# Layer 1 of a two-layer transformer: fifteen gate units computed as seven half-size products with their sums on VectorE, and 32 modulation tiles moved into the projections of layer 2

## The reference

```
m_lat = silu(c) @ w_mod + b_mod            # 6 x 1024 values a layer: shifts, scales, gates
m_ctx = silu(c_ctx) @ w_mod + b_mod
u_lat = h_lat * (1.0 + sc1) + sh1          # and u_ctx alike from m_ctx
pl, pc = u_lat @ w_in, u_ctx @ w_in        # queries, keys, values; pl[10], pc[10] are gate logits
# branches a, b, c, d: attention, Fourier mix, window attention, neighbourhood attention
gates = sigmoid(gate_logits)               # 4 branches x 1024 features
merged = sum over i of gates[i] * (branches[i] @ w_branch[i])
y = merged @ w_out
```

## Time and profile before

| | us |
|---|---|
| median of three executions | 2863.95 (2862.65 to 2864.39) |
| the profiled execution | 2864.46 |
| its span | 2862.6 |
| TensorE busy in the span | 2722.6 (95%) |
| VectorE busy | 1350.7 (47%) |
| ScalarE busy | 436.0 (15%) |

### The profile page before, as it was taken

The page is one execution under the profiler, slowest core; times in us unless marked ns, Lnnn a source line. Parts: engine busy times, 40 slices in busy tenths (PEclk is TensorE's granted clock), DMA queues, the critical chain, the costliest instruction groups (busy, mean ns, idle before and its releaser), DMA issues.

```text
span 2862.6 us, 42389 instructions
## 1 busy us (share of the span) xinstructions
PE 2722.6 (95%) x17586; PEld 1977.2 (69%) x17586; DVE 1350.7 (47%) x2753; ACT 436.0 (15%) x873; POOL 75.4 (3%) x137
## 2 busy tenths in 40 slices
PE   7999999998899899999988998899999999999998
PEld 3544444576666567788644444488788998988997
DVE  3856656442222233785411111179734764843763
ACT  0222220210000012231100000011422211122110
POOL 0100002000000000000100000000000000000000
PEclk9999999999999999999999999999999999999999
DMA  9623339379999985233899999954232444333441
GB/s 377 202 103 122 122 128 356 121 317 421 420 407 421 421 348 165 100 115 148 331 421 421 420 384 421 421 203 160 100 134 104 175 163 147 135 140 116 162 162 45
DMA packets 114765, 685.48 MB, mean 239 GB/s; under 512 B 20752, under 2 KB 22032, under 8 KB 39712
## 3 DMA queue, kind: packets, MB, share of 16 engines
q1 hardware_dynamic: 84144, 600.79, 53.1%
q0 software_dynamic: 16992, 69.54, 6.7%
q10 hardware_dynamic: 13456, 12.59, 1.7%
HBM read 679.46 MB, written 3.41 MB: 239 GB/s over the span
## 4 chain that ended last, share of the span: by engine, by line
PE 37%; DMA 14%; DVE 1%; issue 0%; ACT 0%; SPq 0%; DVEq 0%; ACTq 0%
PE ps L780 14%; DMA ring<-units 14%; PE ps L752 11%; PE ps L1527 2%; PE ps L1346 2%; PE ps L1222 2%; PE ps L1488 1%; DMA early_values<-arena 1%; PE ps L1358 0%; PE ps L1378 0%; PE ps L1088 0%; PE ps L815 0%; PE ps L789 0%; PE ps L798 0%; PE ps L1276 0%
## 5 line engine op out<-in xcount | busy, mean ns | idle before, releaser
L1222 PE MATMUL ps<-ring,arena 128*32 128x256 f32 x2928 | 359.8, 382 | 45.9 <-DMA ring<-units 44.4
L1207 PE MATMUL ps<-ring,arena 128*64 128x256 f32 x2960 | 339.3, 381 | 45.3 <-DMA ring<-units 45.1
L1207 PEld LDWEIGHTS ps<-ring,arena 128*64 128x64 f32 x2960 | 227.0, 137 | 148.7 <-issue 65.5
L1222 PEld LDWEIGHTS ps<-ring,arena 128*32 128x32 f32 x2928 | 175.2, 109 | 222.5 <-DMA ring<-units 90.9
L752 PE MATMUL ps<-h,ring 128*128 128x256 f32 (+1 forms) x992 | 246.0, 408 | 3.2 <-ACT h L1706 2.1
L1047 PE MATMUL ps<-u,ring 128*128 128x512 f32 (+1 forms) x544 | 235.1, 586 | 0.5 <-DVE arena L2345 0.5
L752 PEld LDWEIGHTS ps<-h,ring 128*128 128x128 f32 x992 | 186.7, 190 | 61.3 <-issue 34.7
L1047 PEld LDWEIGHTS ps<-u,ring 128*128 128x128 f32 x544 | 102.6, 191 | 126.7 <-issue 125.1
L2681 DVE COPY u<-ps 32x512 f32<-32x512 f32 (+1 forms) x128 | 70.9, 554 | 209.9 <-PE ps L1222 116.9
L752 PE MATMUL ps<-arena,ring 128*128 128x256 f32 x640 | 139.5, 379 | 1.3 <-DVE arena L3115 1.3
L752 PEld LDWEIGHTS ps<-arena,ring 128*128 128x128 f32 x640 | 121.4, 190 | 18.1 <-DVE arena L3008 1.7
(11 more groups left out here) (501 smaller groups left out, 3958.3 us busy)
## 6 DMA issues: line engine op xcount, KB each, us to landing
ring<-units SPq DMA_DIRECT2D x568, 1024.0 KB, 13.4
slots<-turned_mod POOLq DMA_DIRECT2D x62, 512.0 KB, 5.2
arena<-turned_mod POOLq DMA_DIRECT2D x18, 512.0 KB, 11.2
arena<-quarters ACTq DMA_DIRECT2D x32, 256.0 KB, 2.9
arena<-units POOLq DMA_DIRECT2D x7, 1024.0 KB, 7.2
h<-tokens SPq DMA_DIRECT2D x4, 512.0 KB, 12.2
arena<-neighbours ACTq DMA_DIRECT2D x32, 64.0 KB, 8.8
arena<-tokens ACTq DMA_DIRECT2D x1, 2048.0 KB, 14.2
```

What stands on the lines that cost most here:

```text
L1207: last = nc.tensor.matmul(ps[j * slots:(j + 1) * slots, bank, lo:lo + UC], lhsT[:, kt, 0:slots], row_of(w[j], kt), start=(kt == 0), stop=( ...
L1222: last = nc.tensor.matmul(ps[j % 4 * slots:(j % 4 + 1) * slots, banks[j // 4], 0:UC], lhsT[:, kt, 0:slots], row_of(w[j], kt), start=(kt == ...
```

## The change

Gate units 1 to 15 of layer 1 (512 tokens) are made by `gate_products`: the unit's eight row tiles are split in two halves, its 256 columns in two, and the 512 tokens in latent and context. Seven products of 4 matmuls with 256 columns each take the place of 16 matmuls with 512 columns. They use four banks, two of which (`wb`) also take the quarter's product, so that one waits for `gates_added`. VectorE sums each unit's weights one chunk ahead (`first_wide_sums`, `last_wide_sums`), the tokens once, and adds the results into `gate` in three steps (`early_blocks`, `add_fifth`, `late_blocks`). The sums lie in slots 4 to 7 of the ring, so units 16 to 34 go through slots 0 to 3 alone, and units 36 to 39 are loaded after the last merge.

The 32 tiles for the latent condition alone leave the chunks of layer 1. They are made at the nine places of layer 2's `prepare` (`MOD_AGAIN`), from a copy of the condition that is written to memory at the start and loaded back behind the parked unit 15; their loads stand at the end of GpSimd's program for layer 1, and only the three places of `slots` are left. Of the 48 other tiles, seven are made after `merge(15)`, ahead of the `w_out` residuals; `MOD_MIX` has one tile in each of chunks 0 to 11 and three in each of 12 to 15. The diff (declarations, the removed table `tile_places` and the matching removed lines are left out):

```diff
-MOD_MIX = (1,) + 10 * (3,) + (3, 10, 10, 9, 0)
+MOD_MIX = 12 * (1,) + 4 * (3,)
+MOD_AGAIN = (3, 4, 4, 4, 4, 4, 4, 4, 1)
+GATES, NARROW = 15, 35
+def slot_of(n):
+    return n % (RING // 2) if GATES < n < NARROW else n % RING
...
+        late_conditions = part(13824, 1, D)
...
+        wide_token_sums = [part(1024 * (i % 2), 4, S, of=ring[:, 4 + i // 2, :]) for i in range(4)]
+        wide_weight_sums = [[part(4 * P * i, 4, P, of=ring[:, 7 - q, :]) for i in range(4)] for q in range(2)]
+        gate_blocks = gate.rearrange("p j n -> p (j n)")
+        first_product_kept = small[:, 512:512 + S]
...
+            for n in range(2 * RING, NARROW + 5):
+                if n < 2 * RING + RING // 2:
+                    sp.wait_ge(units_used, n - RING + 1)
+                elif n <= NARROW:
+                    sp.wait_ge(units_used, n - RING // 2 + 1)
+                else:
+                    sp.wait_ge(merged_step, 16)
+                sp.dma_start(ring[:, slot_of(n), :], units[n]).then_inc(loaded[n % RING], 16)
+            gaps = [NARROW + 5] + [n + RING for n in units_to_parks()] + [n_units]
...
-            modulation_tiles(0, MOD_LATE + MOD_SLOTS)
-            pool.wait_ge(mixed, 24)
-            modulation_tiles(MOD_LATE + MOD_SLOTS, MOD_TILES)
+            pool.dma_start(ap["late_conditions"], conditions[0][0:1, 0, :]).then_inc(conditions_stored, 16)
+            modulation_tiles(0, MOD_BOTH)
+            pool.wait_ge(conditions_stored, 16)
             for l in range(DEPTH):
                 if l == 0:
-                    pool.wait_ge(mod_taken, MOD_TILES)
+                    pool.wait_ge(mod_taken, MOD_BOTH)
...
+                    pool.dma_start(late_conditions[:, 0, :], bass.AP(ap["late_conditions"].tensor, 0, [[0, P], [1, D]]))\
+                        .then_inc(conditions_loaded, 16)
...
+                if l == 0:
+                    modulation_tiles(MOD_BOTH, MOD_TILES)
...
+                def gate_products(c):
+                    w = unit()
+                    s, t = wide_weight_sums[c % 2], wide_token_sums
+                    def product(bank, half, lhsT, rhs):
+                        for k in range(4):
+                            last = nc.tensor.matmul(ps[:, bank, half * S:(half + 1) * S], lhsT[:, k, :], rhs[:, k, :],
+                                                    start=(k == 0), stop=(k == 3))
+                        return last
+                    pe.wait_ge(gate_kept, 2 * c)
+                    product(gb + 1, 0, w[:, 0:4, 0:P], u[:, 0:4, 0:S]).then_inc(wide_first_ready, 1)
+                    product(gb, 0, w[:, 4:8, 0:P], u[:, 4:8, 0:S])
+                    pe.wait_ge(wide_tokens_summed, 1)
+                    pe.wait_ge(wide_weights_summed, c)
+                    product(gb, 1, s[1], t[1]).then_inc(wide_early_ready, 1)
+                    attend(2 * c)
+                    pe.wait_ge(merged_step, c)
+                    product(wb + 1, 1, s[0], t[0]).then_inc(wide_fifth_ready, 1)
+                    product(wb, 1, s[2], t[2])
+                    product(wb, 0, s[3], u[:, 4:8, S:]).then_inc(wide_late_ready, 1)
+                    pe.wait_ge(wide_fifth_added, c)
+                    product(wb + 1, 0, w[:, 4:8, P:UC], t[3]).then_inc(units_used, 1)
...
+                    elif chunk:
+                        gate_products(chunk)
...
+                    elif l == 0:
+                        pe.wait_ge(gates_added, chunk)
...
+                    if l == 0 and chunk:
+                        exps(2 * chunk)
+                        act.wait_ge(wide_first_ready, chunk)
+                        A(first_product_kept, ps[:, gb + 1, 0:S], ACT.Copy).then_inc(wide_first_kept, 1)
+                        next_quarter(chunk)
+                        copies(2 * chunk)
+                        exps(2 * chunk + 1)
+                        copies(2 * chunk + 1)
+                        count.skip(units_used, 1)
+                        act.wait_ge(gates_added, chunk)
+                        A(gate[:, :, 0:T], gate[:, :, 0:T], ACT.Tanh, scale=0.5).then_inc(gate_kept, 2)
...
+                if l:
+                    dve.wait_ge(conditions_loaded, 32)
+                    modulated_tiles["from"] = late_conditions
 
                 def beside(place):
-                    if l == 0:
-                        modulation_tiles(MOD_PREPARE[place])
+                    modulation_tiles((MOD_AGAIN if l else MOD_PREPARE)[place])
...
+                first, second, third, fourth = [gate_blocks[:, n * S:(n + 1) * S] for n in range(4)]
+                def first_wide_sums(c):
+                    n, to = GATES + c, wide_weight_sums[c % 2]
+                    w = ring[:, slot_of(n), :].rearrange("p (k c) -> p k c", c=UC)
+                    dve.wait_ge(loaded[n % RING], 16 * (n // RING + 1))
+                    dve.wait_ge(units_used, max(n - 1, GATES))
+                    v.tensor_tensor(to[0], w[:, 0:4, P:UC], w[:, 4:8, P:UC], ALU.add).then_inc(dve_step, 1)
+                    v.tensor_tensor(to[2], w[:, 0:4, 0:P], w[:, 0:4, P:UC], ALU.subtract)
+                    dve.wait_ge(dve_step, at(dve_step))
+                def last_wide_sums(c):
+                    n, to = GATES + c, wide_weight_sums[c % 2]
+                    w = ring[:, slot_of(n), :].rearrange("p (k c) -> p k c", c=UC)
+                    link(v.tensor_tensor(to[1], to[0], w[:, 0:4, 0:P], ALU.subtract))
+                    v.tensor_tensor(to[3], w[:, 4:8, 0:P], to[1], ALU.subtract).then_inc(wide_weights_summed, 1)
+                def early_blocks(chunk):
+                    dve.wait_ge(merged_step, chunk)
+                    dve.wait_ge(wide_first_kept, at(wide_first_kept))
+                    dve.wait_ge(wide_early_ready, at(wide_early_ready))
+                    link(v.tensor_tensor(gate[:, :, 0:S], ps[:, gb, :].rearrange("p (a n) -> p a n", n=S),
+                                         wide(first_product_kept, [P, 2, S]), ALU.add))
+                def add_fifth():
+                    dve.wait_ge(wide_fifth_ready, at(wide_fifth_ready))
+                    v.tensor_tensor(second, third, ps[:, wb + 1, S:], ALU.add).then_inc(wide_fifth_added, 1)
+                def late_blocks():
+                    dve.wait_ge(wide_fifth_added, at(wide_fifth_added))
+                    dve.wait_ge(wide_late_ready, at(wide_late_ready))
+                    link(v.tensor_tensor(gate_blocks[:, S:3 * S], gate_blocks[:, S:3 * S], ps[:, wb, :], ALU.add))
+                    dve.wait_ge(units_used, at(units_used))
+                    count.skip(units_used, -1)
+                    link(v.tensor_tensor(fourth, third, ps[:, wb + 1, S:], ALU.add))
+                    v.tensor_tensor(third, third, ps[:, wb + 1, 0:S], ALU.add).then_inc(gates_added, 1)
...
-                        softmax(2 * chunk)
+                        softmax(2 * chunk, (lambda: first_wide_sums(chunk + 1)) if chunk < 15 else None)
+                        if chunk == 0:
+                            x, s = u, wide_token_sums
+                            link(v.tensor_tensor(s[0], x[:, 0:4, S:], x[:, 0:4, 0:S], ALU.subtract))
+                            link(v.tensor_tensor(s[1], x[:, 4:8, S:], s[0], ALU.subtract))
+                            v.tensor_tensor(s[2], x[:, 4:8, S:], x[:, 0:4, S:], ALU.subtract)
+                            v.tensor_tensor(s[3], x[:, 4:8, 0:S], s[1], ALU.subtract).then_inc(wide_tokens_summed, 1)
...
                         modulation_tiles(MOD_MIX[chunk] // 2, chunk)
                         if 2 * chunk < len(pairs):
                             keep(2 * chunk - 1)
-                        softmax(2 * chunk + 1)
+                        if chunk < 15:
+                            last_wide_sums(chunk + 1)
+                        if chunk:
+                            early_blocks(chunk)
+                            softmax(2 * chunk + 1, add_fifth)
+                            late_blocks()
+                        else:
+                            softmax(2 * chunk + 1)
                         modulation_tiles(MOD_MIX[chunk] - MOD_MIX[chunk] // 2, chunk)
...
                 merge(15)
+                if l == 0:
+                    modulation_tiles(MOD_BOTH - sum(MOD_PREPARE) - sum(MOD_MIX), 16)
```

More of the change, by code:

```diff
@@ L77 @@
 MOD_TILES = 80
-MOD_LATE = 51
-def tile_places(early, late):
-    used, last, places = {}, {}, []
-    for j in range(MOD_TILES):
-        s = j % early if j < MOD_LATE else (j - MOD_LATE) % (early + late)
-        used[s] = used.get(s, 0) + 1
-        places.append((s, used[s], last.get(s, -1)))
-        last[s] = j
-    return places
-TILE_PLACES = tile_places(MOD_SLOTS, 6)
-MOD_PREPARE = (2, 3, 4, 2, 2, 2, 2, 0, 0)
-MOD_MIX = (1,) + 10 * (3,) + (3, 10, 10, 9, 0)
+MOD_PREPARE = (2, 3, 4, 2, 2, 2, 2, 0, 0)
+MOD_MIX = 12 * (1,) + 4 * (3,)
[3 more added lines that the diff above has]
+    return n % (RING // 2) if GATES < n < NARROW else n % RING
 def constants():
@@ L346, in build @@
```

(30 more changed lines are left out.)

25 lines of the change are left out of this document (16 added, 9 removed).

## The result

The changed kernel took 2873.56 us (median of 6 runs, 2869.21 to 2876.56) beside 2863.97 us for the kernel before (6 runs, 2862.65 to 2866.3): a ratio of 1.0032, 95% interval 1.0021 to 1.0043. It is 9.6 us slower, 0.3%. Five more runs of it, taken beside the last version of experiment 7, had a median of 2874.07 us, 1.0041 [1.0028, 1.0055] of before. The first profiled execution (2869.21 us) was the fastest of the six, so I read a second one too (2873.09 us).

What follows compares the result with a forecast made beforehand. TensorE was taken to bound layer 1's chunks, with VectorE's work hidden in layer 2's prepare until it misses a date. 2864.46 - 21.4 + 0.5 + 22.0 + 1.8 = 2867.4, about 2867 us, range 2854 to 2880.

Steps and rivals of the forecast that it cites:

- likeliest case: Whole kernel: stall of 16 to 25 us and saving of 19 to 23 cancel, 2861 to 2872 us; chance 0.50.
- slower by loads: Layer 2's prepare: reloads of 5.5 us make the stall 30 us, time 2875; chance 0.15 beyond the forecast's own edge.
- Its own sign of being wrong: Profile after: a stall under 14 or over 30 us, or TensorE waiting for VectorE inside layer 1's chunks.
- Layer 1, -21.4: Layer 1's mixing: seven shorter products per gate unit, with changed waits, save 21.4 us in all.
- The two guesses in the sum: Layer 1: 2.0 us given back from waits for ScalarE's copies, 0.5 us allowed as loss in chunks 4 and 5.
- slower by VectorE in layer 1: Layer 1's chunks: VectorE's late dates lose 1 us in each of 11, saving 10, time 2878; chance 0.15.
- +0.5 for the extra issue: Start of layer 1: GpSimd's store of the condition ahead of the first tile counts in full, +0.5 us.
- The tiles behind `merge(15)`: End of layer 1's mixing: seven tiles take 17 us of VectorE, hidden behind `w_out`.
- The stall, 22.0: Layer 2's prepare: VectorE's chain of tiles and reloads ends at 1185.6 against 1163.55, so mixing starts 22 us late.
- Two bounds beside the sum: Layer 2's stall: 13 us with all reloads at 3.5 us and no crowding, 8 with none waiting.
- faster: Whole kernel: tiles land in 3.5 us, stall 13, saving 24, time 2856; decides under a 13.6 us stall; chance 0.15.
- The half clock, 1.8: Layer 2's first gate unit: after the stall TensorE's rows run at half clock, +1.8 us.

Runs made afterwards that it cites:

- experiment 7: Changed kernel's gate units, 22 tiles left in layer 2's gaps, five places; last version moves some tiles and reorders reloads against `planned`: 2844.96 us, 0.9939 of before.
- gates_only: Changed kernel without the 32 late tiles of layer 2 and their loads, output not the reference's: 2841.14 us, 0.9926 of the kernel before.
- planned: Changed kernel's gate units, but 58 tiles made in layer 1 and 22 in layer 2's gaps, with five places: 2851.54 us, 0.9963 of the kernel before.
- tiles_only: Kernel before with only the tiles moved as in the change, its gate units as before: 2900.52 us, 1.0131 of the kernel before.
- no_reloads: Changed kernel loading only the first three of the 32 late tiles, all computed, output not the reference's: 2849.93 us, 0.9957 of the kernel before.
- fill_half: Changed kernel with filling products on TensorE ahead of layer 2's first gate unit raised from 3 to 58: 2872.79 us, ratio 1.0032.
- fill_stall: Changed kernel with filling products on TensorE ahead of layer 2's first gate unit raised from 3 to 108: 2889.77 us, one run.

## Why the prediction was right or wrong

**The forecast as a whole.** 2867 against 2873.56: on the slower side of its likeliest case, inside the range, and slower by more than 0.2%, where I gave 0.38. Its own case ended at 2872 and a stall of 25; what happened is the rival "slower by loads", stall 30 and 2875, to which I gave 0.15. Its own sign of being wrong, a stall over 30, came in the second trace (31.0) and was just missed in the first (29.3). That the median stayed this near is in part luck: beside the 1.7 us of full clock in layer 1, both traces have 1.1 to 1.5 us less between `w_out` and the start of layer 2 (594.9 and 595.3 us against 596.4), as TensorE's waits for the ring there fell from 45.1 to 43.7 and 43.1 us. With the same layer 1 `gates_only` took 596.2 us and waited 45.3, so this moves between executions.

**Layer 1, -21.4: right.** The saving of the change itself in the trace is 22.8. The units took 12.25 us where the earlier trace rows gave 12.09, the bare wait 1.13 instead of 1.2. The two guesses in the sum were 1.4 short together: ScalarE's waits gave back 4.3 - 1.4 = 2.9 where I had 2.0, and the 0.5 us allowed for chunks 4 and 5 wasn't needed. The `gates_only` run, whose VectorE has fewer tiles in layer 1 as in the change, measures the whole of it, with the extra issue, as -21.5 against -20.9. The rival "slower by VectorE in layer 1" fell; VectorE even had room for a tile more in chunks 1 to 3 and 8 to 11 (`planned`).

**+0.5 for the extra issue: too small to see.** The start of mixing moved between 140.2 and 143.0 us from trace to trace. I put that down to when single tiles landed; no run shows it.

**The tiles behind `merge(15)`: hidden, as worked out.** VectorE waited once, and its fold was done 2.9 us ahead of TensorE, as before (522.29 - 519.39).

**The stall, 22.0: the term that was mis-sized.** It is 2.94 + 26.84 - 0.51 = 29.3 us in one trace and 2.68 + 28.83 - 0.51 = 31.0 in the other. The chain was the right one, and most of its links held. Of the 7.3 us that the first trace has more, 1.1 are the first keys and values, copied by 1085.49, which is 1112.3 before the shift of layer 2 by 26.8 us, where I had 1111.2; 1.0 lies in VectorE's other work; and 5.2 are waits for reloads, 22.9 instead of 7 x 2.33 + 1.4 = 17.7. Of these 5.2 the first group alone has 4.4: it waited 8.1 us (8.0 in the other trace) instead of 3.7. The other six waited 14.8 us together, and 14.0 was due. So the wrong step is "1.4 more for the first of them, whose reloads meet the crowded queues", put on top of "lands 4.4 us later, the median from 100 to 160 us". The reloads that the first group waited for were used 8.8 to 10.4 us after their issue (issued at 1080.18, 1082.37 and 1087.05, used at 1089.00, 1091.55 and 1097.48), the last one of the seven groups 3.6 us after it (1157.95 to 1161.58).

I took the price of a load from a stretch with a DMA share of 0.36 (100 to 160 us) and carried it, with 1.4 us for all crowding, to one in which ring, parked unit, constants, bias rows and condition come in at once. The earlier trace rows showed 0.49 as a mean over 79 us. The windows of the kernel before, in three pieces, would have shown me that its first 18 us are full (the first two pieces; the DMA share stands ahead of the last number):

```profile
1084.00:1102.00 18.00, 17.89 (x72) 10.99 (x70) 6.66 (x17) 0.60 (x1) 4.87 (x8) 1.00 0.98 308
1102.00:1127.00 25.00, 25.00 (x126) 20.20 (x125) 6.77 (x11) 4.45 (x6) 0.00 (x0) 1.00 0.53 168
```

In the changed kernel 0.94 and 1.08 stand there, for 43 us. That these transfers are what slows the reloads is read from the shares; no run took them away. The earlier trace rows showed landings of 10 to 13 us right there, and I used them for the first three tiles only. A second date was missed too: the copy of `four` stands behind the crowded group, so TensorE lost 2.94 us already at 1099.5.

Two bounds beside the sum don't follow from its terms. With reloads of 3.5 us and no crowding they give 1111.2 + 7 x 6.27 + 19.7 + 3.3 - 1163.55 = 14.5, not 13, and with no load waited for 4.5, not 8; the 11 from a load of 3.2 us should likewise be 12.4. What makes it 8, waits for TensorE that the tiles can't fill, was said but not added up; `no_reloads` has 8.15 - 0.51 = 7.6, so 8 was near. And at a saving of 21.4 the "faster" rival begins at a stall of 2858.2 - 2864.46 + 21.4 - 0.5 - 1.8 = 12.8, not 13.6.

**The half clock, 1.8: right in size**, 5.56 - 3.72 = 1.84 and 6.32 - 3.72 = 2.60. It doesn't grow with the stall: 2.92 us behind 28.6 us (`tiles_only`), 3.02 behind 8.2 (`no_reloads`), 1.69 behind 2.3 (`fill_half`).

**The Trainium skill**, "DMA: Bandwidth & Descriptors", "Anatomy of one DMA", gives 2.0 us plus the bytes at 436 GB/s, an estimate of 3.2 us for such a load. The shortest of the 32 landed in 3.6 us, the median in 5.4 and the longest in 16.4; the measurement decides, and the figure is a floor here.

## What to carry to other kernels

Take the price of a load from the stretch in which it will run, and look at the DMA share there in pieces of 10 or 20 us, not as one mean. Work that is moved to an idle engine has to be cut to the gaps between that engine's dates, one by one: here 32 tiles in even groups cost 30 us and 22 in the right gaps nothing, while the ten that went back to layer 1 cost 3.6 us in its late chunks. And where an engine issues transfers ahead of its own work, loads that others put in flight can hold up that work.

## What the runs showed of the hardware

- ScalarE's issuing of 16 loads of 64 KB rows took 26.2 us with three tiles of 512 KB in flight on GpSimd's queue and 38.0 with five; a quarter's load took 1.1 us to issue in the one case and 4.5 in the other. In the kernel before, with no tiles in flight, the 16 took 21.7 us. Whether it is the number of transfers or their bytes wasn't tried.
- A gap of TensorE of 2.31 us (behind 25.2 us of filling products) was followed by 16 rows in 5.41 us, one of 26.84 by the same rows in 5.56; after 2.40 us idle at the start of layer 1's mixing, 16 rows took 7.13 us in the changed kernel and 8.83 in `fill_stall`, whose program is the same up to there. So short gaps sometimes cost the half clock and sometimes don't; what decides is open.
